# Reordering three attention groups and moving a normalisation beside one of them, in a two-layer hybrid encoder on one core

## The reference

```python
h = rms_norm(x, ln1_g[l]) * (1.0 + sc1) + sh1
cols = h @ w_in[l]                       # split over four head groups a, b, c, d
y_a = mla_mixer(...)                     # group a: dense attention, 4 heads
y_b = swa_mixer(...)                     # group b: +-128 tokens, 4 heads, a sink logit
y_c = diff_mixer(...)                    # group c: 4 heads, two softmax maps per head
y_d = hyena_mixer(...)                   # group d: long convolutions
x = x + g1 * (concat([y_a, y_b, y_c, y_d]) @ w_out[l])
h = rms_norm(x, ln2_g[l]) * (1.0 + sc2) + sh2
x = x + g2 * hier_moe(h, ...)            # top 2 of 32 experts
```

```python
p1 = softmax(q1 @ k1.T * scale);  p2 = softmax(q2 @ k2.T * scale)
o = (p1 - lam * p2) @ v
o = rms_norm(o, norm_g) * (1.0 - lambda_init)     # per head, over 64 values
```

## Time and profile before

| what | value |
|---|---|
| median of three runs | 1690.1 us (1688.35 to 1690.55) |
| profiled execution, its own time | 1678.52 us |
| its span, first to last instruction | 1676.7 us |
| TensorE busy | 1373.4 us, 82% |
| VectorE busy | 617.6 us, 37% |
| ScalarE busy | 370.6 us, 22% |
| GpSimd busy | 269.2 us, 16% |
| mean granted TensorE clock | 0.929 |

### The profile page before, as it was taken

The page is one execution under the profiler, slowest core; times in us unless marked ns, Lnnn a source line. Parts: engine busy times, 40 slices in busy tenths (PEclk is TensorE's granted clock), DMA queues, the critical chain, the costliest instruction groups (busy, mean ns, idle before and its releaser), DMA issues.

```text
span 1676.7 us, 18442 instructions
## 1 busy us (share of the span) xinstructions
PE 1373.4 (82%) x6748; PEld 775.2 (46%) x6748; DVE 617.6 (37%) x1444; ACT 370.6 (22%) x835; POOL 269.2 (16%) x250
## 2 busy tenths in 40 slices
PE   2779999898969589888988999998869779987731
PEld 0244655565544245444444564565544345544420
DVE  3462523256733511333153342246761432111111
ACT  0221112445521111111202112344540211111101
POOL 0000210000000053332220120000000124333211
PEclk9779999999989699999988999999989879999986
DMA  7621021267243789999943122234033669999933
GB/s 234 250 77 40 11 93 74 89 231 249 90 174 126 277 300 315 408 407 404 373 166 107 50 91 76 75 144 173 13 131 130 263 232 326 402 400 404 393 125 113
DMA packets 98608, 336.75 MB, mean 201 GB/s; under 512 B 28370, under 2 KB 33106, under 8 KB 73272
## 3 DMA queue, kind: packets, MB, share of 16 engines
q1 hardware_dynamic: 74712, 305.52, 46.7%
q0 software_dynamic: 15072, 16.85, 4.5%
q10 hardware_dynamic: 8736, 13.21, 2.2%
HBM read 324.08 MB, written 28.98 MB: 211 GB/s over the span
## 4 chain that ended last, share of the span: by engine, by line
PE 67%; DVE 14%; ACT 7%; issue 5%; DMA 3%; POOL 2%; SPq 1%; POOLq 0%; DVEq 0%; ACTq 0%
PE bank L493 62%; ACT pr_r L1333 2%; PE bank L747 2%; PE bank L842 2%; DVE pr_r L1963 2%; DVE pr_r L1822 1%; ACT pr_r L1380 1%; DVE pr_r L1966 1%; DMA big<-in_ada_w_dram 1%; DVE pr_r L1685 1%; POOL small L1451 1%; PE bank L597 1%; SPq L985 1%; ACT ht_r L1312 1%; DVE small L1820 1%
## 5 line engine op out<-in xcount | busy, mean ns | idle before, releaser
L493 PE MATMUL bank<-big,pr_r 128*64 128x256 f32 (+2 forms) x3192 | 451.8, 402 | 65.1 <-issue 25.1
L493 PEld LDWEIGHTS bank<-big,pr_r 128*64 128x64 f32 (+1 forms) x3192 | 269.3, 152 | 218.8 <-issue 108.7
L493 PE MATMUL bank<-big,ht_r 128*128 128x512 f32 (+2 forms) x832 | 330.1, 548 | 1.5 <-ACT ht_r L1346 1.5
L493 PEld LDWEIGHTS bank<-big,ht_r 128*128 128x128 f32 x832 | 155.0, 190 | 145.2 <-issue 137.6
L493 PE MATMUL bank<-big 128*128 128x256 f32 (+4 forms) x496 | 175.5, 492 | 27.9 <-ACT big L1317 10.5
L1516 POOL DMA_INDIRECT x_rows<-ht_r,slot_i x64 | 101.8, 1591 | 324.8 <-DVE ht_r L1969 289.0
L493 PEld LDWEIGHTS bank<-big 128*128 128x128 f32 (+2 forms) x496 | 94.4, 202 | 78.1 <-issue 34.2
L1963 DVE TENSOR_TENSOR pr_r<-pr_r,bank 64x256 f32<-64x256 f32 x65 | 27.5, 423 | 247.5 <-ACT pr_r L1380 236.1
L1380 ACT ACTIVATE pr_r<-bank 64x256 f32<-64x256 f32 x64 | 24.1, 377 | 408.5 <-PE bank L493 408.5
L1450 POOL TENSOR_SCALAR small<-small 128x1 f32<-128x1 f32 (+2 forms) x20 | 7.9, 396 | 561.3 <-DVE small L1847 334.0
L1969 DVE SCALAR_TENSOR_TENSOR ht_r<-bank,mix_r,mod 128x512 f32<-128x512 f32 x65 | 48.8, 751 | 132.6 <-PE bank L493 132.6
(11 more groups left out here) (296 smaller groups left out, 1254.5 us busy)
## 6 DMA issues: line engine op xcount, KB each, us to landing
big<-in_moe_w_gate_dram SPq DMA_DIRECT2D x63, 1024.0 KB, 15.7
big<-in_moe_w_up_dram SPq DMA_DIRECT2D x63, 1024.0 KB, 21.4
big<-in_moe_w_down_dram SPq DMA_DIRECT2D x63, 1024.0 KB, 23.9
big<-in_ada_w_dram SPq DMA_DIRECT2D x16, 3072.0 KB, 11.4
big<-in_w_in_dram SPq DMA_DIRECT2D x4, 3072.0 KB, 14.2
big<-in_w_out_dram SPq DMA_DIRECT2D x4, 2048.0 KB, 8.1
mod<-in_ada_b_dram SPq DMA_DIRECT2D x12, 512.0 KB, 9.9
big<-in_w_in_dram SPq DMA_DIRECT2D x2, 2048.0 KB, 8.1
```

The lines of the kernel that those rows point to most:

```text
L493: return nc.tensor.matmul(o, l, r, start=start, stop=stop)
```

## The change

The groups are worked in the order a, c, b. Group c's norm is split in two pieces inside VectorE's list, one behind the last tile of c (`LAST_C`, output 31) and one three tiles later. The column blocks of a and c are transposed before those of b, and TensorE waits for the last tile (`O47`) only ahead of block 2. Group c's queries are stored like its keys, in two slices of 128 rows that hold four maps each, and a score product reads the 32 rows of its map from both. `qT_c` is no longer cleared. The square's scratch moves to where group c's keys were. The chunks stay behind the same output numbers.

```diff
-        qT_c = at(ht_r, 0, 8, S)
+        qT_c = at(ht_r, 0, 2, S)
...
         for h in range(NH):
             for qt in range(NT):
+                outs.append(("c", h, qt, [len(maps), len(maps) + 1]))
+                maps += [("c", h, qt, 0), ("c", h, qt, 1)]
+        for h in range(NH):
+            for qt in range(NT):
                 outs.append(("b", h, qt, [len(maps)]))
                 maps.append(("b", h, qt, 0))
-        for h in range(NH):
-            for qt in range(NT):
-                outs.append(("c", h, qt, [len(maps), len(maps) + 1]))
-                maps += [("c", h, qt, 0), ("c", h, qt, 1)]
+        A_MAPS, B_MAPS = NH * NT, 3 * NH * NT
+        LAST_C = 2 * NH * NT - 1
...
                             i = 2 * h + m
-                            mm(A.bank(f"S{n}")[:, :], qT_c[:, i, q], kT_c[:, i // 4, :]).then_inc(ready_a, 1)
+                            r = slice(32 * (i % 4), 32 * (i % 4) + 32)
+                            mm(A.bank(f"S{n}")[:, :], qT_c[r, i // 4, q], kT_c[r, i // 4, :]).then_inc(ready_a, 1)
...
                 pe.wait_ge(mix_ready, l + 1)
-                for j in range(6):
+                for j in (0, 1, 4, 5, 2, 3):
+                    if j == 2:
+                        taken(pe, f"O{len(outs) - 1}")
                     b = A.bank(f"xT{j}")
...
-                taken(pe, "xT5")
+                taken(pe, "xT3")
...
                     if e == 2 and l + 1 < DEPTH:
                         sp.wait_ge(mix_ready, l + 1)
+                        taken(sp, f"O{len(outs) - 1}")
                         load_attention(l + 1)
...
-                act.wait_ge(padded, 2 * l + 2)
+                act.wait_ge(padded, l + 1)
                 b = R.take("kTb")
...
                 for j in range(2):
                     b = R.take(f"cT{j}")
-                    for i in range(4):
-                        last = A_(qT_c[32 * i:32 * i + 32, 4 * j + i, :], b[32 * i:32 * i + 32, :], ACT.Copy,
-                                  scale=DIFF_SCALE)
-                    last.then_inc(taken_a, 1)
+                    A_(qT_c[:, j, :], b[:, :], ACT.Copy, scale=DIFF_SCALE).then_inc(taken_a, 1)
...
-                for j in range(6):
+                for j in (0, 1, 4, 5, 2, 3):
                     b = R.take(f"xT{j}")
                     A_(mixT[:, j, :], b[:, :], ACT.Copy).then_inc(taken_a, 1)
...
-                done(g, "c3512")
-                g.memset(qT_c, 0.0).then_inc(padded, 1)
                 g.wait_ge(dss_ready, l + 1)
...
+                c_out = [mix_tok[:, t, 512:768].rearrange("p (h c) -> p h c", h=NH) for t in range(NT)]
+                sq = ar(7168 + 2048, NT, NH, 64)
+
+                def square_sums():
+                    for t in range(NT):
+                        last = TT(sq[:, t], c_out[t], c_out[t], ALU.mult)
+                    step(last)
+                    nc.vector.tensor_reduce(dss.rearrange("p (t h) -> p t h", t=NT), sq, X, ALU.add).then_inc(dss_ready, 1)
+
+                def norm():
+                    v.wait_ge(drs_ready, l + 1)
+                    for t in range(NT):
+                        last = TT(c_out[t], c_out[t], drs[:, 4 * t:4 * t + 4].unsqueeze(2).to_broadcast([P, NH, 64]), ALU.mult)
+                    step(last)
+                    for t in range(NT):
+                        last = TT(c_out[t], c_out[t], gd.unsqueeze(1).to_broadcast([P, NH, 64]), ALU.mult)
+                    last.then_inc(mix_ready, 1)
...
                         took(TS(mix_tok[:, qt, c:c + 64], b[:, lo:lo + 64], mx[:, m0:m0 + 1], None, ALU.mult))
+                        if n == LAST_C:
+                            square_sums()
+                        if n == LAST_C + 3:
+                            norm()
```

More of the change, by code:

```diff
@@ L740, in layer @@
                         elif g == "b":
-                            pe.wait_ge(prob_b, 16 * l + ms[0] - 15)
+                            pe.wait_ge(prob_b, 16 * l + ms[0] - B_MAPS + 1)
                         else:
-                            pe.wait_ge(diff_ready, 16 * l + n - 2 * NH * NT + 1)
+                            pe.wait_ge(diff_ready, 16 * l + n - A_MAPS + 1)
                         b = A.bank(f"T{n}")
@@ L1325, in layer @@
                             w = band(qt)[1] - band(qt)[0]
-                            act.wait_ge(swa_s, 16 * l + n - 16 + 1)
+                            act.wait_ge(swa_s, 16 * l + n - B_MAPS + 1)
                             pr = prob[:, n % 4, 0:w]
                             A_(pr, pr, ACT.Exp, bias=nm[:, n:n + 1], accum_out=rs[:, n:n + 1])
-                            A_(esink[:, n - 16:n - 15], sink[:, h:h + 1], ACT.Exp, bias=nm[:, n:n + 1]).then_inc(prob_b, 1)
+                            A_(esink[:, n - B_MAPS:n - B_MAPS + 1], sink[:, h:h + 1], ACT.Exp, bias=nm[:, n:n + 1]).then_inc(prob_b, 1)
                         else:
                             b = R.take(f"S{n}")
-                            act.wait_ge(nm_ready, 48 * l + (n + 1 if g == "a" else n - 16 + 1))
+                            act.wait_ge(nm_ready, 48 * l + n + 1)
                             A_(prob[:, n % 4, :], b[:, :], ACT.Exp, bias=nm[:, n:n + 1],
@@ L1814, in layer @@
                             g, h, qt, ms = outs[n]
-                            o = n - 2 * NH * NT
+                            o = n - A_MAPS
                             taken(v, f"S{ms[1]}")
@@ L1828, in layer @@
                         if g == "b":
-                            v.wait_ge(prob_b, 16 * l + m0 - 15)
-                            step(TT(den[:, m0 - 16:m0 - 15], rs[:, m0:m0 + 1], esink[:, m0 - 16:m0 - 15], ALU.add))
-                            step(nc.vector.reciprocal(mx[:, m0:m0 + 1], den[:, m0 - 16:m0 - 15]))
+                            v.wait_ge(prob_b, 16 * l + m0 - B_MAPS + 1)
+                            mine = slice(m0 - B_MAPS, m0 - B_MAPS + 1)
+                            step(TT(den[:, mine], rs[:, m0:m0 + 1], esink[:, mine], ALU.add))
+                            step(nc.vector.reciprocal(mx[:, m0:m0 + 1], den[:, mine]))
                         else:
@@ L1840, in layer @@
                         mod_take(n)
-                c_out = [mix_tok[:, t, 512:768].rearrange("p (h c) -> p h c", h=NH) for t in range(NT)]
-                sq = at(pr_r, 0, NT, NH, 64)
-                for t in range(NT):
-                    last = TT(sq[:, t], c_out[t], c_out[t], ALU.mult)
-                step(last)
-                nc.vector.tensor_reduce(dss.rearrange("p (t h) -> p t h", t=NT), sq, X, ALU.add).then_inc(dss_ready, 1)
-                v.wait_ge(drs_ready, l + 1)
-                for t in range(NT):
-                    last = TT(c_out[t], c_out[t], drs[:, 4 * t:4 * t + 4].unsqueeze(2).to_broadcast([P, NH, 64]), ALU.mult)
-                step(last)
-                for t in range(NT):
-                    last = TT(c_out[t], c_out[t], gd.unsqueeze(1).to_broadcast([P, NH, 64]), ALU.mult)
-                last.then_inc(mix_ready, 1)
                 for half in range(2):
```

## The result

The changed kernel takes 1657.81 us in the median of four runs (1654.31 to 1660.0), beside 1689.22 us (1681.28 to 1690.55) for the kernel before on the same chip: ratio 0.9828, 95% interval 0.9806 to 0.9851. The forecast was 1660. The profiled executions stand closer together than the medians, at spans of 1658.2 and 1676.7 us, only 18.5 apart; the first experiment says why.

A forecast was written before the change was run, and what follows sets the result against it. It took the third group as bound by a VectorE-ScalarE circle, the second by VectorE, with TensorE waiting at front and tail. Terms of -15.8 and -13.8 us, say -30, took 1690.1 to 1660 us, range 1649 to 1676.

The forecast's parts named there:

- front: Before each layer's attention: no memset, two copies for eight, full clock in the first scores; -7.3 us (-4.8 to -7.3).
- tail: Last attention product to output projection: the norm's 9.57 us leave the path; -10.5 us a layer (-8.5 to -10.9).
- norm beside b, with its clock: Second group worked: norm on VectorE costs +2.5 and +5.0 us by layer, pauses that lower the clock +1.0 each.
- chunks and seams: Between first and last tile: chunks -2.6 and -3.1 us by layer, seams +1.1 each.
- the clock in the second layer: Beside group b: the norm's two pieces make pauses in which TensorE's clock falls; +1.0 us (0 to 3).
- Chunks: Modulation chunks move into the third group, which has spare TensorE time; -2.6 and -3.1 us by layer (0 to -5).
- the overlap of row quarters: Group c's scores: two pairs from different row quarters run together, giving TensorE 0.86 us more to spare per tile.
- Seams: Group ends and entries: the third group's last tiles lose the early finish of an empty pipe; +1.1 us a layer.
- Half the gain (1670): Attention parts: clock still falls at front and tail, no row-quarter overlap, norm costs its whole 5.5 us; 1670 us, chance 0.20.
- that rival: Third group: 32-row scores leave TensorE idle, clock falls, pitch 4.5 us; slower, 1718 us, chance 0.07 including a mild form.
- The experts' transfers: First layer's experts: weight stream does not move, so that layer's attention gain is lost; 1676 us, chance 0.05.

The follow-up runs named there:

- the first experiment: The kernel before, run again with no edit, against itself: ratio 1.0014 (0.9998 to 1.0029), span 1693.4 us.
- the front alone: Kernel before with only two query slices, 32-row scores and no memset; group order and norm stay: ratio 0.9924, -12.8 us.

## Why the prediction was right

The sum was -15.8 and -13.8 us; the table above has -18.5 and -13.6. That the second layer meets to 0.2 us is luck: tail and chunks came 1.7 us better there, the norm 1.6 worse. Its terms beside what they measured, with the norm's share from the run that has it at the end and the chunks as what is left between first and last tile:

| term, first / second layer | forecast | measured |
|---|---|---|
| front | -7.3 / -7.3 | -7.4 / -7.0 |
| tail | -10.5 / -10.5 | -11.7 / -11.7 |
| norm beside b, with its clock | +3.5 / +6.0 | +4.1 / +7.6 |
| chunks and seams | -1.5 / -2.0 | -3.5 / -2.5 |

**Front: right in each part.** From the last copy to TensorE's first score it is 5.1 us less (12.2 to 7.2), where 4.8 were forecast, and from there to the first tile 2.3 less (8.7 to 6.4), where 2.5 stood for the clock. The run with the memset splits the first again: 1.2 the wait, 3.9 the copies (forecast 1.09 and 3.7).

**Tail: right, 1.2 us short, and past its own bound of -10.9.** The forecast left 4.4 us between the last product and the projection; it is 3.6. ScalarE's copies start 0.5 us after the last product and run at a pitch of 0.48 us, which is all that is left. The rest of the difference is that the table counts from the last tile's scaling, which now comes 0.7 us after its product, not 0.3.

**Norm: the mechanism right, the size too small.** What was mis-sized is above all the clock in the second layer: +1.0 was forecast, and 2.3 to 3.0 us lie in the tiles around the two pieces, with two falls, each after one piece. I also took half a microsecond off the 5.5 us of VectorE for hiding, and 0.2 was hidden (2.6 + 2.7 = 5.3). What a fall costs shows in the first layer, 1.0 to 1.1 us beside the run with the gains on GpSimd, which had the same wait and no fall; why the clock fell in one and not in the other, no run tells. The chunk after output 35 did cover most of the second piece there, as forecast: it costs 0.5 us beside the run with the norm at the end, 2.7 in the second layer.

**Chunks: right, and the overlap of row quarters is what was in doubt.** A chunk with a sum costs 3.26 us in group c (5.26 + 5.05 less two plain steps), forecast 2.9; one without 1.98, forecast 1.9. With scores from 128 rows these are 3.97 and 2.33, so the overlap is worth 0.7 and 0.35 us a chunk. By the Trainium skill ("TensorE: Matmul & The Clock Gate", Part 3) row quarters run concurrently; the trace agrees, four instructions in 1.13 us for 1.88. The same skill's "TensorEngine Tiling (Array Packing)", Key Properties, says that a change of tiling mode drains TensorE. No cost of it shows, the pitch is 3.52 to 3.53 us with two such changes in each tile and without; but TensorE waits 0.92 us in each of these tiles, and a smaller cost would be hidden there.

**Seams: the step that failed.** The +1.1 held that the end loses what an empty pipe gave the third group. It loses nothing: b's last three tiles come at 2.03, 0.89 and 0.71 us, 2.5 under two plain steps of 2.08, just what c's last ones gave before. In its place group a pays: 47.4 and 47.2 us for its 16 tiles instead of 45.8 and 45.7, and the steps that grow are its last three, beside which maps of c are already made. The list shows that these maps now stand there; the forecast had half a microsecond of the other sign. With scores from 128 rows it is 46.7 in both layers, so that 0.5 to 0.7 of it come with the 32 rows; why, no run told. The two errors nearly cancel in the second layer, which is luck. In the first, 1.6 of the 2.0 us by which chunks and seams came out better have another cause: before, the last two steps of the attention took 6.1 us there (4.65 + 1.45) and not 4.5, with TensorE at half clock from 471.2 to 474.7, and the forecast read this end in the second layer.

**The rivals.** Half the gain (1670) falls with the clock in front and the overlap, though its norm of 5.5 was nearer than mine in the second layer. The clock never fell between c's first and last tile in any profile with the order a, c, b (28.87 of 37 us busy), and the pitch of 4.5 us at which that rival decides stayed away. Where c comes last it did fall there: for 3.4 us at its end in the first layer of both profiles of the kernel before, and at its entry (410.8) with the front alone. The experts' transfers swallowed nothing: from the first to the last expert of the first layer it is 259.0 us in the changed kernel and 259.1 in the repeat of the kernel before. The forecast kept the 11.6 us between profile and median and so expected a span of 1647; the changed kernel's profile has 1658.2, beside its median. The profile of the kernel before was an unusually short one, by 5.4 + 4.1 + 4.1 = 13.6 us outside the attention; only its median was a fair base. The range's low end, 1649, should have read 1650 (1690.1 - 40); nothing hangs on it.

**Left open.** What holds ScalarE and SyncE up at expert 4 was not tried, nor what decides whether the clock falls after a wait. Outside the attention the same instructions differ by up to 9 us between profiles (start-up 300.6 to 309.6; last expert of the first layer to the second `c` projection 233.7 to 240.0), so that distances of one stage, which repeat to 0.1 us where the clock does the same, could be settled here and differences of kernels under 3 us could not.

## What to carry to other kernels

Work moved from the end of a stage to beside a group that hangs on the same engine costs its full length there, and what the pauses do to the clock on top (5.3 and 2.3 to 3.0 us in the second layer here); the move still pays if at the end everybody waited for it (11.7 us), and pays more on an engine that is idle in that group (look for single instructions that slow down beside it). Chunks of another engine's work belong into the group with spare time on that engine, or right beside such a pause: moving them took 13.6 us from first to last tile in two layers, the norm's whole move to GpSimd 10.0 (both beside the changed kernel's repeat). Before two profiles are subtracted, cut both at events that they share, and look for stretches that differ where nothing was changed.

## What the runs showed of the hardware

- Two score products that read different quarters of 32 rows and write different banks start 14 ns apart by their single records and take 1.13 us for four instructions, where the same from 128 rows take 1.88.
- At expert 4 ScalarE starts 2.2 to 3.2 us behind TensorE's transposes instead of 0.1, in both layers of every profile but one, in all kernels, and SyncE's load starts with it (606.92 in the changed kernel). In the first layer of the changed kernel TensorE is at half clock for 3.4 us soon after (from 609.5).
- The same wait does not always end the full clock. Behind the norm's first piece TensorE waited 3.6 us in the first layers of the changed kernel and its repeat, and the clock fell for 3.4 us; it waited 3.61 us in those of the runs with the gains on GpSimd (chunks in place, and all in group c), and the clock stayed up. The wait of 1.43 us before the first scores was followed by half clock once in 22 times.
- GpSimd multiplies 128x256 values in 0.58 us each (2.33 for four) beside a busy VectorE. VectorE's addition of two values per row, both from the tile `small`, takes up to 0.63 us beside it instead of 0.16 (0.35 to 0.55 with only the gains moved); its masking from a bank and its maxima keep their 0.56 and 0.55 us.
